# Moving the exponentials of the local attention one step ahead in ScalarE's order

## The reference, cut to what matters

```python
h = rms_norm(x, norm1_g[l]) * (1.0 + sc1) + sh1
q, k, v, gu, gv, ga, gb = jnp.split(h @ w_in[l], splits, axis=-1)
y_a = sliding_window_attention(q, k, v, positions, sinks[l], rel_bias)
y_b = spatial_gating(jax.nn.gelu(gu), jax.nn.gelu(gv), gm_ln_g[l], gm_ln_b[l], gm_w_s[l], gm_b_s[l])
merged = jax.nn.sigmoid(ga) * (y_a @ p_a[l]) + jax.nn.sigmoid(gb) * (y_b @ p_b[l])
...
# in sliding_window_attention
m = jnp.maximum(jnp.max(s, axis=-1, keepdims=True), sink)
p = jnp.exp(s - m)
p = p / (jnp.sum(p, axis=-1, keepdims=True) + jnp.exp(sink - m))
o = jnp.einsum('bnhgqs,bnshd->bnqhgd', p.astype(v.dtype), vb)
```

## Time and profile before

| | us |
|---|---|
| median of 3 runs | 2959.91 |
| lowest and highest run | 2957.91 and 2961.19 |
| the profiled execution | 2961.19 |
| its span, first to last instruction | 2959.4 |
| TensorE busy | 2827.7 (96% of the span) |
| VectorE busy | 2235.3 (76%) |
| ScalarE busy | 1485.4 (50%) |
| mean granted TensorE clock | 0.980 of full speed |

### The profile page before, as it was taken

The page is one execution under the profiler, slowest core; times in us unless marked ns, Lnnn a source line. Parts: engine busy times, 40 slices in busy tenths (PEclk is TensorE's granted clock), DMA queues, the critical chain, the costliest instruction groups (busy, mean ns, idle before and its releaser), DMA issues.

```text
span 2959.4 us, 37313 instructions
## 1 busy us (share of the span) xinstructions
PE 2827.7 (96%) x13639; PEld 2360.5 (80%) x13639; DVE 2235.3 (76%) x3019; ACT 1485.4 (50%) x1991; POOL 584.1 (20%) x460
## 2 busy tenths in 40 slices
PE   5989987999999989999999999999999999999998
PEld 3667756888888858776777789999999988888887
DVE  6465647888888862796965599999877658888886
ACT  3353235878888833454552334565766533333332
POOL 0210111111111100000000000233433324444442
PEclk7999998999999999999999999999999999999999
DMA  7554636999999843232334323688989999999995
GB/s 306 171 171 160 213 117 238 368 369 368 363 355 360 308 149 118 87 114 89 118 107 150 113 86 143 231 308 298 368 311 315 326 325 359 370 359 358 361 369 174
DMA packets 201771, 737.90 MB, mean 249 GB/s; under 512 B 24432, under 2 KB 77808, under 8 KB 145008
## 3 DMA queue, kind: packets, MB, share of 16 engines
q1 hardware_dynamic: 124656, 497.12, 46.6%
q0 software_dynamic: 55056, 170.87, 16.7%
q10 hardware_dynamic: 21872, 67.48, 5.9%
HBM read 666.61 MB, written 93.91 MB: 257 GB/s over the span
## 4 chain that ended last, share of the span: by engine, by line
PE 62%; DVE 14%; issue 4%; ACT 3%; DMA 1%; ACTq 0%; DVEq 0%; SPq 0%; POOLq 0%; POOL 0%
PE PS L544 54%; DVE wlo L1889 3%; PE PS L1145 2%; PE PS L1011 1%; DVE hf L2703 1%; PE PS L1023 1%; ACT whi L1221 1%; PE PS L850 1%; DVE hf L2691 1%; DVE oh L2677 1%; ACT HH L1859 1%; DVE cand L2640 1%; DVE cand L2638 1%; PE PS L1002 1%; DVE i L2574 0%
## 5 line engine op out<-in xcount | busy, mean ns | idle before, releaser
L1889 DVE TENSOR_TENSOR wlo<-raw,whi 128x2048 fp32r<-128x2048 f32 x392 | 894.0, 2288 | 297.1 <-ACT whi L1221 275.0
L1221 ACT ACTIVATE whi<-raw 128x2048 fp32r<-128x2048 f32 x392 | 750.8, 1917 | 374.9 <-PE PS L544 320.8
L544 PE MATMUL PS<-HH,whi 128*128 128x512 f32 (+1 forms) x2056 | 786.3, 382 | 22.5 <-ACT HH L1257 9.0
L544 PE MATMUL PS<-HH,wlo 128*128 128x512 f32 (+1 forms) x2056 | 749.6, 365 | 0.0
L544 PE MATMUL PS<-HL,whi 128*128 128x512 f32 (+1 forms) x2056 | 749.3, 364 | 0.0
L544 PEld LDWEIGHTS PS<-HH,whi 128*128 128x128 f32 x2056 | 389.2, 189 | 82.2 <-issue 20.2
L544 PEld LDWEIGHTS PS<-HL,whi 128*128 128x128 f32 x2056 | 389.5, 189 | 46.3 <-issue 7.4
L544 PEld LDWEIGHTS PS<-HH,wlo 128*128 128x128 f32 x2056 | 388.5, 189 | 43.4
L544 PE MATMUL PS<-whi,HH 128*128 128x512 f32 (+1 forms) x896 | 352.7, 394 | 10.7 <-DVE HL L2735 5.4
L544 PE MATMUL PS<-wlo,HH 128*128 128x512 f32 (+1 forms) x896 | 348.5, 389 | 0.0
L544 PE MATMUL PS<-whi,HL 128*128 128x512 f32 (+1 forms) x896 | 348.3, 389 | 0.0
(11 more groups left out here) (434 smaller groups left out, 3897.8 us busy)
## 6 DMA issues: line engine op xcount, KB each, us to landing
raw<-in_moe_dram SPq DMA_DIRECT2D x192, 1024.0 KB, 7.4
raw<-in_u_units_dram SPq DMA_DIRECT2D x64, 1024.0 KB, 6.5
raw<-in_v_units_dram SPq DMA_DIRECT2D x64, 1024.0 KB, 8.7
raw<-in_w_in_dram SPq DMA_DIRECT2D x44, 1024.0 KB, 5.1
raw<-in_w_ada_dram SPq DMA_DIRECT2D x24, 1024.0 KB, 6.0
acts_dram<-sS ACTq DMA_DIRECT2D x64, 384.0 KB, 6.2
gates_dram<-XT ACTq DMA_DIRECT2D x24, 1024.0 KB, 8.3
sS<-acts_dram SPq DMA_DIRECT2D x42, 384.0 KB, 6.6
```

The source lines that it names most:

```text
L544: ins = t.matmul(dst, a, b, start=(first and n == 0), stop=(last and n == 2))
L1221: a.inc(a.e.activation(m.whi[p % HRING][:, :, :], m.raw[RAW_SLOT[load_of(p)]][:, :, :], ACT.Copy), "hi", p)
L1889: v.inc(v.e.tensor_tensor(m.wlo[h][:, :, :], m.raw[RAW_SLOT[load_of(p)]][:, :, :], m.whi[h][:, :, :].bitcast(F32), ALU.subtract), "lo_v", p)
```

## The change

The exponentials of round n are issued by ScalarE in tick 3n and not in tick 3n + 1. They stand ahead of the copies of round n - 1, and ahead of what lies between the two ticks: the Gelu or Tanh of a quarter, or the high part of a unit. TensorE's, VectorE's, GpSimd's and SyncE's lists are the same as before.

```diff
@@ def act_local(a, m):
         if n == 3:
             a.wait_ge("bnst", 3)
             a.inc(s.activation(m.sd4[:, :], m.mv[:, :, 1], ACT.Sqrt, bias=m.epst[:, 0:1]), "sdev")
+        if n < 8:
+            i = n % 2
+            a.wait_ge("negmax", n)
+            for j in range(4):
+                a.inc(s.activation(m.S[:, i, j, :], m.S[:, i, j, :], ACT.Exp, bias=m.nm[:, i, j:j + 1],
+                                   accum_out=m.rs[:, i, j:j + 1]), "expo", n, j)
+            a.wait_ge("sinkd", n)
+            a.inc(s.activation(m.es[:, i, :], m.es[:, i, :], ACT.Exp), "expo", n, 4)
         yield
         if n:
             k = n - 1
@@
                 a.inc(s.activation(m.Pt[:, c2, :, :].rearrange("p j q -> p (j q)"), m.PS[:, (7, 4)[c2], :],
                                    ACT.Copy), "pt", k, c2)
-        if n < 8:
-            i = n % 2
-            a.wait_ge("negmax", n)
-            for j in range(4):
-                a.inc(s.activation(m.S[:, i, j, :], m.S[:, i, j, :], ACT.Exp, bias=m.nm[:, i, j:j + 1],
-                                   accum_out=m.rs[:, i, j:j + 1]), "expo", n, j)
-            a.wait_ge("sinkd", n)
-            a.inc(s.activation(m.es[:, i, :], m.es[:, i, :], ACT.Exp), "expo", n, 4)
         yield
```

## The result

The changed kernel is slower: 2972.79 us median of 7 runs (2966.96 to 2978.40) against 2957.91 us for the kernel before (7 runs, 2953.04 to 2962.75). The ratio, which rests on more runs than these seven (17 of the changed kernel are on record), is 1.0056, 95% interval 1.0042 to 1.0070, which is 16.6 us (12.4 to 20.7); the two medians alone differ by 14.9. The profiled execution took 2970.07 us for a span of 2968.3.

A forecast was written before the change was run, and what follows sets the result against it. TensorE, busy 96% of the span, was taken as the bound; shifts of 5.9 + 2.1 - 1.0 + 1.5 + 2.2 + 0 + 0.7 + 2.2 = 13.6 us on 2959.91 gave 2973.5 us, range 2965 to 2982.

The forecast's parts named there:

- the sum of 13.6 us: Rounds 1 to 7: TensorE's added shifts, 13.6 us in all, the likeliest outcome with chance 0.52, giving 2973.5 us.
- Rounds 1 and 2: TensorE's multiplications with the values wait for the copy `Pt`, 4.8 us and 2.1 us; shift 5.9, then 8.0 us.
- The tail of low clock behind the first wait: After round 1's wait TensorE loses 1.0 to 2.3 us to a lower clock; taken as 1.6.
- The transposes of round 2: TensorE's stall there, for VectorE's division, shrinks from 4.67 to 3.7 us; shift becomes 7.0 us.
- Round 3: Copies end at 212.1 and TensorE comes at 210.6, so it waits 1.5 us; shift 8.5 us.
- Round 5: ScalarE's way with the high part 10.3 us, TensorE's 10.89 us from scores to multiplication; wait taken as 0.
- the stated upper bound: Round 5's wait is at most 1.0 us, if TensorE needs only 9.3 us from scores to multiplication.
- The order of loads and waits: ScalarE's table load taken as running behind the wait; ahead of it, rounds 2 and 3 wait up to 1.3 us less each.
- First stall alone: Rival: only round 1's stall costs, later copies being in time; 5.9 plus about 1 us, 2966 to 2967; chance 0.18.
- More clock lost: Rival: further waits each drop TensorE's clock, 1.0 to 2.3 us each; three add 5, giving 2978.5 us; chance 0.17.
- Hidden: Rival: shift taken back before the experts, or ScalarE's wait not in TensorE's way; 2957 to 2963 us; chance 0.09.
- Faster: Rival: early exponentials let VectorE divide early, ending the stall at 197.65 with its tail; 2951.6 us; chance 0.04.

The follow-up runs named there:

- the control: The kernel before, unchanged, timed and profiled once more against itself: ratio 0.9995 (0.9987 to 1.0004), span 2952.5 us, stretch from scores of round 0 to last multiplication 116.47 us.
- both partial versions: Against the kernel before, exponentials moved in all rounds but round 1: ratio 1.0045, 13.3 us slower; in round 1 alone: 1.0026, 7.7 us slower.

## Why the prediction was right, by its own steps

The direction, the place and the mechanism held in every round. That its median, 2973.5, is only 0.7 us from the measured one is luck: the sum of 13.6 us was too small (14.9 by the medians, 16.6 by the ratio), and the base of three runs, 2959.91, was 2.0 above the later median of 2957.91. The base profile hid the same gap: against it the stretch grew by 132.53 - 118.79 = 13.7, against the control by 16.1. Of the missing 2.5 us, 1.1 are in round 5 and about 0.5 each in round 3, in round 6 and ahead of the first wait.

| round | predicted wait, us | measured |
|---|---|---|
| 1 | 4.8 | 4.64 |
| 2 | 2.1 | 2.09 |
| 3 | 1.5 | 2.97 |
| 4 | 2.2 | 2.02 |
| 5 | 0 (at most 1.0) | 0.77 |
| 6 | 0.7 | 0.90 |
| 7 | 2.2 | 2.02 |

**Rounds 1 and 2** came as worked out (the rows of round 1 give 4.7 us when added up, and not 4.8). The tail of low clock behind the first wait, put at 1.6, is 180.21 - 174.80 = 5.41 us less the control's 3.78, 1.6.

**The transposes of round 2** were to keep a wait of 3.7 us and its low clock. They kept 1.94 and 0.54. What the sum hadn't is a second tail behind the wait of round 2: 196.75 - 191.35 = 5.40 us, where the control has 185.62 - 181.92 = 3.70. It brought TensorE 1.7 us later to the transposes, whose wait shrank by as much.

**Round 3** was mis-sized for the same reason. Without a long wait at the transposes there was no low clock behind them: from 203.62 TensorE needed 211.19 - 2.97 - 203.62 = 4.60 us, where I took 5.94 from the earlier trace rows. ScalarE's side was right (the load behind the wait, at 206.56), so TensorE waited 1.5 longer. Way and wait together are nearly the same, 7.57 us against the 7.44 I had, since the copy sets when the multiplication starts.

**Round 5** makes up the largest part of what the sum lacked. It was taken at 0 because TensorE had needed 10.89 us. The control's 9.30 is the figure that the stated upper bound was made of. The row of 10.89 held a low clock of one execution, as the control shows. The shape of ScalarE's side was right: the high part ran from 240.22, the copies after it.

**The order of loads and waits**: behind the wait, as assumed (185.44 and 206.56, each with the idle time ahead of the load). One load fewer stands in the stretch, six instead of seven, as counted. The rule on table sets in the Trainium skill, "ScalarE: Activation LUTs", section "Table sets: the hidden batching unit", speaks for the change by this one load, and the change cost 16.6 us. The same page of the Trainium skill puts a switch, in its section "What ACT_TABLE_LOAD costs", at load plus drain, 2.66 us. That is not what these rows show: the load at 172.37 begins 0.02 us after the high part's end (170.46 + 1.89), and the Gelu begins at 173.66, 1.29 after the load's start. A switch cost 1.3 us here, and no drain shows.

**The rivals.** First stall alone: refuted by both partial versions. More clock lost: there were two tails and not four, and the old one went. In part this rival was right, since the second tail stood in no term of the sum. Hidden: not so. From the scores of round 0 to the first expert's first transposes (line 850) it is 474.76 - 152.18 = 322.58 us after and 459.74 - 151.08 = 308.66 in the control, 13.9 more. So 2.2 of the stretch's 16.1 us are gone by then, and where is not shown; from there to the end of the span nothing more comes back (2493.5 against 2492.8 us). Faster: its condition, the maximum of round 1 before ScalarE arrives, missed by 5.34 us. On a faster base the change costs about as much, 129.33 - 112.95 = 16.4 us with the square root early and 15.4 with the low parts late.

What adds up to the 16.1 us: new waits 15.4; transposes of round 2 wait 2.2 less; two tails of low clock +1.6 and +1.7; the old one 1.3 less (5.37 us in the control, 4.60 - 0.54 here); the wait of 0.69 ahead of the scores of round 2 gone. That is 14.5. The other 1.6 are small pieces: 0.5 ahead of the first wait (170.16 - 152.18 = 17.98 us, 17.49 in the control), and 0.12 to 0.17 in each of nine later pieces of the way, such as 4.68 against 4.54 us from a late multiplication to the next scores, less 0.3 in the two others. Why TensorE's way without waits is longer by these, no run tells.

## What to carry to other kernels

An instruction that is issued earlier on an engine with a fixed order brings its wait forward with it: look at what stood in the idle time that is now spent waiting, and for whom. The earlier result was worth nothing here: TensorE waited for only one division of VectorE, and ahead of that one VectorE had other work and a wait of its own. The thing to move was that work (7.1 us faster), or the small instruction it waited for (4.7 us faster). And before a term of under 2 us is taken from one execution, profile the kernel before twice.

## What the runs showed of the hardware

TensorE's clock fell behind some short waits and not behind others. Behind the same wait of 4.64 or 4.65 us, the time to the next scores was 5.41, 5.32, 6.08 and 6.75 us in four versions (the change, round 1 only, square root early with the change, low parts late with the change), against 3.78 without the wait, so 1.5 to 3.0 us were lost. Behind a wait of 2.09 to 2.13 us in round 2 it was 5.40 in two of these versions and 3.81 in the last, against 3.70. Behind a wait of 2.01 to 2.04 us in round 4 it was 4.66 to 4.68 in three versions and 6.35 in the one that leaves out round 1. So a wait can cost almost as much again as it lasts.

The amount can't be put down to the version, since each was profiled once and two profiles of the same kernel differ too. Behind the old wait at the transposes of round 2 the kernel before took 5.94 us to the multiplication in one profile and 5.37 in the other, and two versions with the same wait of 4.61 and 4.65 us took 6.84 and 6.20. In the first of the two profiles the clock also fell with no wait at all: it was 0.50 from 226 to 228 us and 0.66 from 228 to 230, with TensorE busy the whole time. What decides it, no run here tells.
